# Differential attention on one core: each tile's turns one tile later, ahead of the scores of a later tile

## What is computed

```python
def differential_attention(q, k, v, lam):
    s = jnp.einsum('bhiqd,bhikd->bhiqk', qb, k) * scale
    s = s - (slopes[:, None, None] * dist[None])[None, :, None]
    p = jax.nn.softmax(s, axis=-1)
    a = p[:, :, 0] - lam * p[:, :, 1]
    return jnp.einsum('bhqk,bhkd->bhqd', a, v)
```

## Time and profile before

| what | us |
|---|---|
| median of three executions | 2527.78 |
| lowest, highest | 2526.22, 2528.99 |
| span of the profiled execution | 2521.2 |
| PE busy | 2496.5 (99%) |
| DVE busy | 1765.8 (70%) |
| ACT busy | 1152.4 (46%) |
| POOL busy | 410.9 (16%) |

### The profile page before, as it was taken

How to read it: one execution, slowest core, us unless ns; L and a number is a source line. 1 busy time by engine, 2 the same in 40 slices (tenths; PEclk the granted TensorE clock), 3 DMA queues, 4 the chain that set the end, 5 groups by cost and what they waited for, 6 DMA issues and landing times.

```text
span 2521.2 us, 34920 instructions
## 1 busy us (share of the span) xinstructions
PE 2496.5 (99%) x12891; PEld 2058.5 (82%) x12891; DVE 1765.8 (70%) x2655; ACT 1152.4 (46%) x2012; POOL 410.9 (16%) x317
## 2 busy tenths in 40 slices
PE   9999999899999999999999999999999999999998
PEld 7888877688888888888888888888888888888887
DVE  6556565656878878666577777777657888887655
ACT  6555654535333333444455454546344333334433
POOL 1001022400332333100000000000002333332000
PEclk9999999999999999999999999999999999999999
DMA  3122253723444444866211111111334444447754
GB/s 130 59 60 77 60 129 99 216 93 117 155 171 163 150 168 167 315 219 211 81 48 49 50 50 50 48 50 72 117 109 144 164 157 162 157 160 255 246 194 152
DMA packets 189171, 332.38 MB, mean 132 GB/s; under 512 B 59728, under 2 KB 67792, under 8 KB 180816
## 3 DMA queue, kind: packets, MB, share of 16 engines
q1 hardware_dynamic: 154208, 320.62, 37.1%
q10 hardware_dynamic: 34800, 9.60, 1.7%
HBM read 238.24 MB, written 91.91 MB: 131 GB/s over the span
## 4 chain that ended last, share of the span: by engine, by line
PE 96%; DVE 2%; ACT 1%; issue 1%; DMA 0%; POOL 0%; ACTq 0%; SPq 0%; DVEq 0%
PE PS L2422 21%; PE PS L2337 19%; PE PS L2339 19%; PE PS L2338 19%; PE PS L2586 5%; PE PS L2518 4%; PE PS L2542 3%; PE PS L2534 1%; PE PS L2489 1%; PE PS L2563 1%; PE PS L2345 1%; PE PS L2436 1%; PE PS L2567 1%; PE PS L2503 1%; PE PS L2479 1%
## 5 line engine op out<-in xcount | busy, mean ns | idle before, releaser
L2422 PE MATMUL PS<-HH,WS 128*128 128x512 f32 x1536 | 516.0, 402 | 3.4 <-DVE HL L1641 2.0
L2422 PEld LDWEIGHTS PS<-HH,WS 128*128 128x128 f32 x1536 | 285.6, 188 | 60.0 <-DVE HL L1641 2.1
L2422 PE MATMUL PS<-HL,WS 128*128 128x512 f32 x768 | 301.9, 393 | 0.0
L2126 DVE TENSOR_TENSOR SPLIT<-RAWI,SPLIT 128x1024 fp32r<-128x1024 f32 x154 | 195.3, 1271 | 148.2 <-ACT SPLIT L1469 147.7
L1469 ACT ACTIVATE SPLIT<-RAWI 128x1024 fp32r<-128x1024 f32 x154 | 163.0, 1060 | 206.8 <-PE PS L2339 151.9
L2337 PE MATMUL PS<-TH,WS 128*128 128x512 f32 x640 | 249.2, 389 | 0.7 <-ACT SIL L1461 0.7
L2338 PE MATMUL PS<-TL,WS 128*128 128x512 f32 x640 | 249.0, 389 | 0.0
L2339 PE MATMUL PS<-TH,WS 128*128 128x512 f32 x640 | 249.0, 389 | 0.0
L2337 PE MATMUL PS<-SPLIT 128*128 128x512 f32 x616 | 240.0, 390 | 0.0
L2339 PE MATMUL PS<-SPLIT 128*128 128x512 f32 x616 | 239.7, 389 | 0.0
L2338 PE MATMUL PS<-SPLIT 128*128 128x512 f32 x616 | 239.6, 389 | 0.0
(11 more groups left out here) (274 smaller groups left out, 4957.9 us busy)
## 6 DMA issues: line engine op xcount, KB each, us to landing
WR<-wstrips SPq DMA_DIRECT2D x224, 256.0 KB, 2.7
RAWI<-ab_scratch SPq DMA_DIRECT2D x154, 256.0 KB, 4.2
ab_scratch<-SIL SPq DMA_DIRECT2D x132, 256.0 KB, 2.0
WD<-wdown SPq DMA_DIRECT2D x22, 1024.0 KB, 7.4
wd_scratch<-WD SPq DMA_DIRECT2D x22, 1024.0 KB, 3.8
RAWI<-wd_scratch SPq DMA_DIRECT2D x88, 256.0 KB, 3.3
UR<-wstrips SPq DMA_DIRECT2D x80, 256.0 KB, 3.1
RAWI<-wdown SPq DMA_DIRECT2D x66, 256.0 KB, 3.8
```

The costliest lines, as they stand in the source:

```text
L2126: e.tensor_tensor(SPLIT[m % 6][:, 1], RAWI[:, m % 4], f(SPLIT[m % 6][:, 0]), ALU.subtract).then_inc(S["ilo"], 1)
L2422: last = e.matmul(ps, wt, xt, start=g == 0, stop=g == 23)
```

## The change

On PE the turn of a tile moves into the next tile's place in the loop and stands there as the first step, ahead of the scores. The scores in that place belong to the tile two further on. ACT's `hi` moves along. DVE's `lo` moves along too: where values follow (`last`, even n) it stands ahead of the table additions, elsewhere behind them as it did. In the last head, tile 6 is turned at the end of its own place, ahead of the sums, and tile 7 at the start of its own. Nothing is computed differently and no buffer is added.

```diff
--- before.py
+++ after.py
@@ -550,6 +550,10 @@
             after = (8 * layer + (g + 1) // NQ, (g + 1) % NQ) if g + 1 < 8 * NQ else None
             last = (P, n - 1) if n else (P - 1, NQ - 1)
             yield P, n, after, last if g and n % 2 == 0 else None, P % 8 < 7
+
+    def before(P, n):
+
+        return [] if (P, n) == (8, 0) else [(15, 7)] if (P, n) == (15, 7) else [(P, n - 1) if n else (P - 1, NQ - 1)]
 
     def score_bank(P, n, m):
         return m if 4 <= P < 7 else 2 * (n % 2) + m
@@ -1385,7 +1389,8 @@
                     y_root(0, KC - 1)
                     e.wait_ge(S["rt_turned"], 1)
                     e.activation(RH[0:64, :], PS[0:64, FILL_BANK, 128:256], ACT.Copy).then_inc(S["rt_high"], 1)
-                hi(P, n, 0, "C")
+                for v in before(P, n):
+                    hi(*v, 0, "C")
                 for m in range(2):
                     if after:
                         exp(*after, m, "C")
@@ -1397,6 +1402,8 @@
                 if n in splits(P):
                     ahead, slot, used = splits(P)[n]
                     w_split(w + ahead, slot, 1, ("fill_done", 6 * P + used))
+                if (P, n) == (15, NQ - 2):
+                    hi(P, n, 0, "C")
                 if not more:
                     for i in SQUARED_AT.get(n, []):
                         y_square(i)
@@ -1979,6 +1986,9 @@
                 first, second = turned_v(P, n)
                 for v in evacuated(P, n):
                     evac(*v, PV_BANK if v == (8, 0) else None)
+                for v in before(P, n):
+                    if last:
+                        lo(*v, 0, "C")
                 for m in range(2):
                     if after:
                         ttr(*after, m)
@@ -1987,7 +1997,9 @@
                     e.wait_ge(S["rt_high"], 1)
                     e.tensor_tensor(RH[64:128, :], PS[0:64, FILL_BANK, 128:256], f(RH[0:64, :]),
                                     ALU.subtract).then_inc(S["rt_low"], 1)
-                lo(P, n, 0, "C")
+                for v in before(P, n):
+                    if not last:
+                        lo(*v, 0, "C")
                 if after:
                     factors(*after)
                     combine(*after)
@@ -2000,6 +2012,8 @@
                                            op1=ALU.mult).then_inc(S["yeps_done"], 1)
                     e.wait_ge(S["yeps_done"], 1)
                     y_mean(0, KC - 1)
+                if (P, n) == (15, NQ - 2):
+                    lo(P, n, 0, "C")
                 for v in first + second:
                     vlo(*v)
                 if n in splits(P):
@@ -2706,9 +2720,10 @@
             for P, n, after, last, more in order(1):
                 first_part, second_part = fills_at(P, n)
                 first, second = turned_v(P, n)
+                for v in before(P, n):
+                    turn(*v, 0, "C")
                 if after:
                     qk(*after)
-                turn(P, n, 0, "C")
                 for v in first:
                     tv(*v, P, n)
                 fills(first_part, P, 1)
@@ -2718,6 +2733,8 @@
                 fills(second_part, P, 1)
                 for v in second:
                     tv(*v, P, n)
+                if (P, n) == (15, NQ - 2):
+                    turn(P, n, 0, "C")
                 if not more:
                     if n == 3:
                         e.wait_ge(S["fill_evac"], 96)
```

## The result

The changed kernel took 2564.07 us (median of 4 runs, 2561.38 to 2565.48), the kernel before beside it 2527.32 us. The ratio is 1.0151, with a 95% interval of 1.0138 to 1.0163: it is slower by 1.5%. The prediction said 2558.5 us in a range of 2540 to 2568.

What follows compares the result with a forecast made beforehand. The prediction took PE to bound the stage, busy 485.98 of 486.00 us. Its terms, 2.2 + 22 + 6.5 = 30.7 us, added to 2527.8 gave 2558.5 us; 8 in 10 between 2540 and 2568.

Steps and rivals of the forecast that it cites:

- Part 1: On PE, the turn in front of the scores: 0.05 us more per place, entry and exit together, +2.2 us.
- Part 2: Values in tiles 2, 4, 6 of heads 8 to 14 wait for DVE's fresh lower part: +22 us.
- the shift: Second exponential, and so combine, weight split and evac, come 0.32 us later; bounds 0 and 0.88.
- Part 3: Head 15, without fills from tile 2 on: waits ahead of values and last turn, +6.5 us, bounds 2 and 10.
- The mark: In head 15, the first spread was to come 7 us later, measured from the scores of tile (15,2).
- The 6.6 us between span and median: Median of the kernel before above its profiled span of 2521.2 us; carried along unchanged into the forecast.
- Cheap entry, no wait: Rival: turns ahead of scores save 0.12 us some 50 times, lower parts come in time; 2521.8 us, chance 0.08.
- T + 1.2: T is the turn's start in the new order; tiles 2 and 6's upper part must start by 1.2 us after.
- Nothing measurable: Rival: entry gain and a few waits cancel, 2523 to 2533 us; chance 0.08.
- The third rival: Tiles 2, 4 and 6 keep waits of 0 to 0.4 us; head 15 and order remain, about 2540 us; chance 0.18.

Runs made afterwards that it cites:

- e5: Changed kernel with ACT's tile upper part ahead of the strip's in heads 8 to 14 and head 15 in the order of before: 2531.03 us, ratio 1.0020.
- e7: e5 with the turn, still one tile later, behind the scores instead of ahead of them: 2558.76 us, ratio 1.0122.
- e6: e5 with DVE's lower part ahead of the table additions in tiles 3 and 7 too: 2538.38 us, ratio 1.0047.
- e1: Changed kernel with ACT's tile upper part ahead of the new strip's in tiles 2, 4, 5 and 6: 2539.89 us, ratio 1.0047.
- e2: Changed kernel with four fills more ahead of the values in tiles 2, 4 and 6: 2549.28 us, ratio 1.0093.
- e8: Kernel before with the turn ahead of the scores in its own tile, not one tile later: 2586.86 us, ratio 1.0231.
- e3: Changed kernel with DVE's lower part behind both table additions in every tile: 2618.36 us, ratio 1.0356.
- e9: Changed kernel with tile (15,6)'s lower part on DVE ahead of the mean of the sums: 2559.62 us, ratio 1.0134.

## Why the prediction was right

**Part 1, the order on PE.** Predicted 0.05 us a tile, and 2.2 in all (by its own count of some 50 places it should have been 2.5). The distances of e5 give 0.05 or 0.06 in tiles 0, 4, 5 and 6, 0.04 in tile 2 and 0 in tile 1, where value turns stand on both sides; e7 shows that it is the order. Tiles 3 and 7 have 0.11 and 0.23: I had written that 16 fills cover the lower part that the next turn needs. They fall short, by about 0.06 us in tile 3 and 0.19 in tile 7, as the timelines in e6 show. So the order itself comes to 0.37 us a head, 2.6 in all, and the term with these two waits to 4.4 instead of 2.2 us. The Trainium skill, TensorEngine Tiling (Array Packing), Tiling Modes, says that a change of tiling mode drains TensorE. The traces agree as far as they can: the entry behind a turn is 0.20 instead of 0.32, as the trace of before had it. Taken alone it would have promised a gain; the exit takes it back.

**Part 2, the values' wait.** Predicted 1.3, 0.8 and 1.1 us in tiles 2, 4 and 6, measured 1.37, 0.78 and 1.16 (the distance to the fill ahead, 1.60, 1.01 and 1.39, less 0.23). The steps hold one by one: evac 0.29 later against the last fill in tile 6 (1.36 behind it instead of 1.07), the strip's upper part 0.72 behind evac, the tile's 0.54 behind that, the lower part 1.04 behind that. A restart costs a little more than the 0.05 I gave it: values stood ready 3.54 behind evac by my sum and started 3.62 behind it. The choice of 0.32 for the shift, and not of 0 or 0.88, is what made the term right; it came from asking what stood in front of the exponential that would no longer stand there. e1 shows the cause by taking it away. In 7 heads these waits are 23.2 us, and the distances without the order's share give 24.4, against 22 predicted.

**Part 3, head 15.** Predicted 6.5 us, with 2 and 10 as bounds, measured 11.0. Here the term was mis-sized, by something that was not in the sum: the granted clock. The idle time ahead of the values of (15,2) is 2.4 us (2.2 predicted), that ahead of (15,4) and (15,6) 1.6 and 1.5 (1.6 and 1.8), that ahead of the last turn 1.6 (1.4). But in (15,2) the 24 matmuls of the values take 4.3 us from first to last instead of 2.8, and from the first spread to the output projection 8.7 us pass instead of 5.7. These 4.5 us lie in the two windows with the granted clock at 0.65 and 0.62, and without them head 15 loses 6.5. Ahead of both PE had been idle: the 2.4 us wait, then the 1.6 and 0.7 us waits of the last turn and of the spread. The mark that the prediction named, the first spread counted from the scores of (15,2), moved from 45.9 to 53.9 us, 8.0 instead of 7; the other 3.0 us come behind it, where the prediction had nothing.

**The sum** was 30.7 us, 36.8 were measured: 2.2 too low in part 1, 2.4 in part 2, 4.5 in part 3, and the stage of the profiled execution lost 3 us more than the medians. The range held, with 4 us to spare. The 6.6 us between span and median that I carried along are not what separates time and span: that is 1.8 us in every run whose both are on record, and the other 4.8 say that the profiled execution of before was faster than the median. This did not touch the forecast, which adds the loss to the median.

**The signs.** A head takes 70.4 us (69.7 predicted, 66.3 before). One sign came out the other way: PE's busy time was to fall by some 25 us and rose by 13.3. The same work is recorded, and what makes it last longer counts as busy: the order and the short waits of tiles 3 and 7 (4.4 us), the lower clock (4.5), and at each wait ahead of the values in heads 8 to 14 about 0.16 us that the view does not call idle (3.4 in 21 waits); the sum, 12.3, is an estimate from the distances above.

**The rivals.** "Cheap entry, no wait" named the point from which it would decide, the upper part at T + 1.2: it started at T + 2.4 in tile (9,6). e5 is this rival made true, and even then no gain appears, so its price of -6 us was wrong as well as its condition; the gain at the entry is real and smaller than the loss at the exit. "Nothing measurable", 2523 to 2533, needed entry gain and waits to cancel, and the changed kernel lies 31 us above it. The third rival, waits of 0 to 0.4, is nearly what e2 shows with four more fills, and it did not happen by itself.

## What to carry to other kernels

Where two engines make their steps in a fixed order, moving a producer later is not paid on the engine that is moved but in the queue of the next: list what stands ahead of the consumer's step on each queue, with its own due time, before trusting the sum of free-engine latencies (3.4 us here, 4.8 to 5.3 in fact). An entry cost read at one edge of a block is half of a price; put the whole stretch together, entry and exit, from places where the same neighbours already meet. And a repair of one wait has to be followed once around the loop: e2 and e6 both moved the wait to another tile.

## What the runs showed that was not expected

- The granted clock fell to its lower level in short stretches, each time during or shortly behind a long idle time of PE: 2.4 us in (15,2) of the changed kernel (0.65 in a window of 4.9 us), 1.6 and 0.7 us ahead of its spreads (0.62 in one of 9 us), 1.9 us in (15,4) of e1 (0.94 over 27 us), 1.7 to 1.8 us four times in heads 8 to 14 of e8, 2.6 us seven times there in e3. It did not follow each one: e3 has 14 such waits in these heads, and e2 and e9 have 2.3 us in (15,2) and keep the upper level. With idle times of up to 1.2 us three times a head it never fell (heads 8 to 14 of the changed kernel, clock 1.00 in 482 us), nor with 1.5 us twice a head (e7).
- How long a wait takes to end depends on the pair. PE's values start 0.10 us behind the end of DVE's lower part, a turn 0.15 behind it, and scores 0.23 or 0.24 behind the end of ACT's exponential. The 24 matmuls of the values take 2.83 us from first to last behind a wait and 2.75 behind a fill without one; but they take 2.83 behind a turn without a wait too (head 15 of the kernel before), so the 0.08 is not a price of the wait alone.
- The waits view put the values' 25 us of waiting down to "issue". The releaser was only to be seen in the timeline, as a lower part that ended 0.1 us earlier each time.
